# Layer 0's key pages turned on VectorE in 32x32 blocks: loads by quarters, new slot and query-tile order

## The chip, the cores and the metric

The kernel runs on one core of one Trainium2 chip. The metric is the device time of one launch in microseconds (us), given as the median of the runs. Engines are named as in the profile: PE (TensorE; PEld is its weight loads), DVE (VectorE), ACT (ScalarE), POOL (GpSimd) and SP (SyncE, which here issues nearly all DMAs). All arithmetic of the part that is changed is in float32.

## What is computed

Two layers of a decoder trunk run as one step for a prompt of 512 tokens and for a sample group of 8 sequences with 8 new tokens each. Every sample sequence has 1024 past tokens in 8 pages of 128, found through a page table. The change touches the attention of layer 0 only, where 8 forgetting ("fox") heads and 4 differential heads (two query/key halves each) attend side by side. Cut from the reference:

```python
def fox_diff_attend(qa, qb, cq, q_pos, ka, va, ck, kb, vb, k_pos, lam, subln0):
    causal = k_pos[None, :] <= q_pos[:, None]
    sa = einsum('bqhd,bkhd->bhqk', qa, ka) * scale
    sa = sa + (cq - ck)                      # sums of the log forget values
    oa = einsum('bhqk,bkhd->bqhd', softmax(where(causal, sa, -inf)), va)
    sb = einsum('bqhcd,bkhcd->bhcqk', qb, kb) * scale
    pb = softmax(where(causal, sb, -inf))
    ob = einsum('bhqk,bkhe->bqhe', pb[:, :, 0] - lam * pb[:, :, 1], vb)
    return concat(oa, rms_norm(ob, subln0) * (1 - LAMBDA_INIT))

# sample group, one sequence: 8 pages of keys and values (128 tokens x 1024), then the 8 new tokens
k_all = concat(cache_k[page_table], k_new); v_all = concat(cache_v[page_table], v_new)
```

A page of keys or values is 128 x 1024 float32, 512 KB. There are 64 of each.

## The kernel before

`FirstAttention` does this attention in 32 slots (the loop variable `x`), four to a sample sequence (`b, k = divmod(x, 4)`); the text calls four slots a batch. Each slot carries one unit of the prompt and a share of one sequence of the sample.

A unit is a pair of heads `p` and a query tile `qt` of 128 prompt tokens; its scores are (qt+1) x 128 wide. `QT_ORDER` sets the order of the query tiles in a pair. The first 16 units are "mixed" (differential heads: two score matrices are blended into one), the last 16 are fox heads (two score matrices each). For unit `x`, PE computes `scores(x)`, DVE the row maximum (`top`), ACT the exponentials (`exps`), DVE the reciprocal sums (`sums`); for mixed units POOL scales and DVE blends (`blend`). One slot later PE transposes the probabilities (`turn(x-1)`), ACT (and DVE, for a fox unit's second head) copies them out of PSUM (`head_out`), and PE multiplies them by the values (`weigh(x-1)`).

Of the sample, a slot takes in two key pages and two value pages. A key page arrives with tokens on the 128 partitions and features along the row. The score product needs features on the partitions, so `turn_keys(g)` lets PE transpose the page in eight 128x128 pieces into two PSUM banks (`RING`), and `keys_out(g)` copies them to SBUF, one bank by ACT and one by DVE. `score_page` then multiplies a turned page by the 128 query rows of the sequence (16 heads x 8 tokens) with 32-column tiles of PE, and `weigh_page` does the same for a value page with the transposed probabilities. The two RING banks also serve the transposes of probabilities, of the sample's probabilities (`turn_probs`) and of its output (`turn_o`).

SP issues the loads in one order: key page `g` waits until page `g-5` has been turned (five places), then value page `h = g - 11` waits until page `h-4` has been used (four places). Before each of them SP reads the page number from a table in SBUF. There are three places for turned keys.

The order of a slot on PE is written out by hand in `tensor`: scores, first key page turned, first value page, `turn(x-1)`, one page scored, second key page turned, second value page, another page scored, `weigh(x-1)`; the fourth slot of a batch scores four pages, the first none. After the last slot the last sequence's probabilities are turned and its eight value pages weighed, and the output projection of layer 0 follows.

Of the kernel before, what the change touches and what calls it, by code (L numbers as in the profile page):

```python
# [18 lines left out]
P = 128  # L19
# [8 lines left out]
KC = D_MODEL // P  # L28
# [40 lines left out]
def constant_table():  # L69
# [13 lines left out]
    row_head, row_query = i // DEC_SEQ, i % DEC_SEQ  # L83
# [4 lines left out]
    put("selections", selections)  # L88
    put("new_mask", np.where(h8[None, :] <= row_query[:, None], 0.0, NEG))
# [1246 lines left out]
class FirstAttention:  # L1336
    
    KEY_PLACES, VALUE_PLACES, TURNED_PLACES = 5, 4, 3
    QT_ORDER = (2, 1, 3, 0)
# [4 lines left out]
    def __init__(self, nc, K, mem, qp, kp, vp, qs, ks, vnew, retired, next_tile):  # L1344
# [3 lines left out]
                 "turned_a", "turned_b", "emptied_a", "emptied_b", "chain", "pool_chain",  # L1348
# [12 lines left out]
        self.knew, self.snew, self.st = sb("knew", [P, KC, DEC_SEQ]), sb("snew", [P, DEC_SEQ]), sb("st", [P, 2, 10])  # L1361
        self.squares = sb("squares", [P, DIFF, SEQ])
# [18 lines left out]
        self.fills_after_key = {}  # L1381
        self.fill_of_second_probs = {}
        self.fill_of_second_head = {}
# [21 lines left out]
    def tensor(self, pe):  # L1405
        K, S = self.K, self.S
        filled = [0, 0]
        turned, emptied = (S["turned_a"], S["turned_b"]), (S["emptied_a"], S["emptied_b"])

        def ring(x):  # L1410
            if filled[x]:
                pe.wait_ge(emptied[x], filled[x])
            filled[x] += 1
            return self.RING[x]
# [16 lines left out]
        def turn(u):  # L1431
            p, qt = self.units[u]
            for i in range(1 if self.mixed(u) else 2):
                bank = ring(i)
                if self.mixed(u):
                    pe.wait_ge(S["blended"], self.count(u + 1, True))
                for j in range(qt + 1):
                    ins = pe.transpose(bank[:, j * P:(j + 1) * P], self.probs[:, u % 2, i, j * P:(j + 1) * P], K.c("ident"))
                ins.then_inc(turned[i], 1)
                if i:  # L1440
                    self.fill_of_second_head[u] = filled[1]
            self.head_fills = (filled[0], filled[1])

        def weigh(u):
            p, qt = self.units[u]
            pe.wait_ge(emptied[0], self.head_fills[0])
            if not self.mixed(u):
                pe.wait_ge(emptied[1], self.head_fills[1])
# [18 lines left out]

        def turn_keys(g):
            pe.wait_ge(self.k_in[g % self.KEY_PLACES], 16 * (g // self.KEY_PLACES + 1))
            for x in range(2):  # L1470
                bank = ring(x)
                for c in range(4):
                    at = (4 * x + c) * P
                    ins = pe.transpose(bank[:, c * P:(c + 1) * P], self.keys[g % self.KEY_PLACES][:, at:at + P], K.c("ident"))  # L1474
                ins.then_inc(turned[x], 1)
            self.fills_after_key[g] = filled[1]
            self.key_fills[g] = (filled[0], filled[1])
# [9 lines left out]
        def score_page(b, j):  # L1487
# [10 lines left out]
            pe.wait_ge(emptied[0], self.key_fills[g][0])  # L1498
            pe.wait_ge(emptied[1], self.key_fills[g][1])
# [4 lines left out]
        def score_news(b):  # L1504
            news = ring(1)[:, 0:DEC_SEQ]
            pe.matmul(news, K.fox_sel[32:32 + 2 * FOX, :], self.bias_rows[:, PAST_LEN:KEYS], start=True, stop=True)
            score_into(news, lambda c: self.knew[:, c, :]).then_inc(turned[1], 1)

        def turn_probs(b):
            for half in range(2):  # L1510
                bank = ring(half)
                pe.wait_ge(S["s_exped"], 3 * b + (1, 3)[half])
# [3 lines left out]
                ins.then_inc(turned[half], 1)  # L1516
            self.probs_fills[b] = (filled[0], filled[1])
            pe.transpose(ring(1)[0:DEC_SEQ, 0:P], self.s_probs[:, PAST_LEN:KEYS], K.c("ident")).then_inc(turned[1], 1)
            self.fill_of_second_probs[b] = filled[1]
# [49 lines left out]
        for x in range(self.SLOTS + 1):  # L1569
            b, k = divmod(x, 4)  # L1570
            if k == 1 and b >= 2:
                turn_o(b - 2)
# [1706 lines left out]
```

## Time and profile before

| | us |
|---|---|
| median of 3 runs | 1894.41 (1892.2 to 1894.65) |
| the profiled execution, its own time | 1891.96 |
| its span, first to last instruction | 1890.2 |
| layer 0's attention: first key page issued to last value page weighed | 229.4 to 515.6 |
| PE busy over the span | 1707.6 (90%) |
| DVE, ACT, POOL busy over the span | 853.5, 603.2, 151.1 |
| mean granted TensorE clock | 0.957 |

The profile is one execution seen by the hardware profiler. A line of it names the source line, the engine, the operation, what is written and read, and how often; "idle before" is the time the engine stood still just ahead of such instructions, and the releaser is what ended it. PE's matmuls overlap, so the distance from one start to the next tells more than the length of one. TensorE's clock is granted at one of two levels, 1.00 (2.4 GHz) and 0.50 (1.2 GHz); a stretch in which it changed shows a value between. The DMA share is the mean busy share of the core's 16 DMA engines.

### The profile page before, as it was taken

To read this page: it belongs to the slowest core of one execution; us is meant where nothing else is said; L and a number is where in the kernel's file an instruction comes from. 1 tells how busy PE (TensorE), PEld (TensorE's weight loads), DVE (VectorE), ACT (ScalarE), POOL (GpSimd) and SP (SyncE) were. 2 spreads that over 40 slices of the span, in tenths; PEclk is the share of its full clock that TensorE was granted. 3 is DMA by queue.
4 is the path that set the end of the run, shared out by engine and by line. 5 is a ranking of instruction groups with operands and counts; after the bars stand their busy time and mean duration, and the time that the engine had idled before them with its cause. 6 is when DMAs were issued, how large, how long until landed. Compare 5 with 4: busy or idle time off the path is not lost. (4 is left out here: it accounts for less than half of the span.)

```text
span 1890.2 us, 32284 instructions
## 1 busy us (share of the span) xinstructions
PE 1707.6 (90%) x12454; PEld 1422.2 (75%) x12462; DVE 853.5 (45%) x1570; ACT 603.2 (32%) x1275; POOL 151.1 (8%) x303
## 2 busy tenths in 40 slices
PE   5999788998798999999998788687888999999998
PEld 3787565665478999799987576355457999889987
DVE  4446455445435322323224978985545232233323
ACT  3325344433223321112213344554333232112220
POOL 1222223111000000000000012110000000000000
PEclk9999899999898999999998899798999999999999
DMA  5232278766632222333321112101752322233221
GB/s 183 68 117 57 86 265 278 269 218 222 205 101 67 76 79 84 87 104 83 105 76 59 48 45 48 46 1 47 217 137 67 89 68 83 84 90 85 70 84 67
DMA packets 177043, 201.61 MB, mean 107 GB/s; under 512 B 21650, under 2 KB 131538, under 8 KB 176914
## 3 DMA queue, kind: packets, MB, share of 16 engines
q1 hardware_dynamic: 167634, 189.39, 32.6%
q10 hardware_dynamic: 9200, 10.24, 1.7%
q8 instruction: 81, 1.33, 0.3%
q14 instruction: 48, 0.39, 0.1%
q0 software_dynamic: 80, 0.26, 0.1%
HBM read 190.77 MB, written 9.08 MB: 106 GB/s over the span
## 5 line engine op out<-in xcount | busy, mean ns | idle before, releaser
L211 PE MATMUL ps<-feat_lo,w_hi 128*128 128x288 f32 x1408 | 416.5, 296 | 7.4 <-PEq L2451 3.8
L213 PE MATMUL ps<-feat_hi,w_hi 128*128 128x288 f32 x1408 | 416.5, 296 | 0.0
L212 PE MATMUL ps<-feat_hi,w_lo 128*128 128x288 f32 x1408 | 416.1, 296 | 0.0
L193 DVE TENSOR_TENSOR w_lo<-w_raw,w_hi 128x2048 fp32r<-128x2048 f32 x96 | 220.1, 2292 | 339.5 <-ACT w_hi L187 339.4
L187 ACT ACTIVATE w_hi<-w_raw 128x2048 fp32r<-128x2048 f32 x96 | 183.6, 1913 | 348.8 <-PE ps L219 334.9
L211 PEld LDWEIGHTS ps<-feat_lo,w_hi 128*128 128x128 f32 x1408 | 265.7, 189 | 8.6 <-issue 4.4
L212 PEld LDWEIGHTS ps<-feat_hi,w_lo 128*128 128x128 f32 x1408 | 265.7, 189 | 0.0
L213 PEld LDWEIGHTS ps<-feat_hi,w_hi 128*128 128x128 f32 x1408 | 265.5, 189 | 0.0
L2551 DVE TENSOR_TENSOR f_prod<-f_silu,ps 128x576 f32<-128x576 f32 x44 | 33.2, 754 | 361.1 <-ACT f_silu L2530 361.1
L211 PE MATMUL ps<-w_lo,feat_hi 128*128 128x512 f32 (+1 forms) x448 | 182.4, 407 | 13.5 <-DVE feat_lo L2403 5.5
L212 PE MATMUL ps<-w_hi,feat_lo 128*128 128x512 f32 (+1 forms) x448 | 177.9, 397 | 0.0
L213 PE MATMUL ps<-w_hi,feat_hi 128*128 128x512 f32 (+1 forms) x448 | 177.8, 397 | 0.0
L2530 ACT ACTIVATE f_silu<-ps 128x576 f32<-128x576 f32 x44 | 28.7, 652 | 429.6 <-PE ps L213 429.6
L212 PE MATMUL ps<-w_hi,f_act_lo 128*128 128x512 f32 x352 | 137.0, 389 | 0.0
L211 PE MATMUL ps<-w_lo,f_act_hi 128*128 128x512 f32 x352 | 137.0, 389 | 0.0
L213 PE MATMUL ps<-w_hi,f_act_hi 128*128 128x512 f32 x352 | 136.9, 389 | 0.0
L211 PEld LDWEIGHTS ps<-w_lo,feat_hi 128*128 128x128 f32 x448 | 88.6, 198 | 32.3 <-issue 14.4
L213 PEld LDWEIGHTS ps<-w_hi,feat_hi 128*128 128x128 f32 x448 | 87.9, 196 | 17.9
L212 PEld LDWEIGHTS ps<-w_hi,feat_lo 128*128 128x128 f32 x448 | 88.6, 198 | 16.1
L1474 PE MATMUL ps<-const,places 128*128 128x128 f32 x512 | 70.7, 283 | 13.4 <-ACT a_probs_t L1618 8.6
L213 PEld LDWEIGHTS ps<-w_hi,f_act_hi 128*128 128x128 f32 x352 | 66.1, 188 | 13.7
L211 PEld LDWEIGHTS ps<-w_lo,f_act_hi 128*128 128x128 f32 x352 | 66.1, 188 | 13.6
(340 smaller groups left out, 2386.4 us busy)
## 6 DMA issues: line engine op xcount, KB each, us to landing
places<-in_cache_l_k_dram SPq DMA_DIRECT2D x64, 512.0 KB, 4.5
places<-in_cache_l_v_dram SPq DMA_DIRECT2D x64, 512.0 KB, 5.1
w_raw<-in_w_gate_dram SPq DMA_DIRECT2D x44, 512.0 KB, 4.0
w_raw<-in_w_up_dram SPq DMA_DIRECT2D x44, 512.0 KB, 5.3
w_raw<-in_w_in_dram SPq DMA_DIRECT2D x18, 1024.0 KB, 5.2
w_raw<-in_w_down_dram SPq DMA_DIRECT2D x16, 1024.0 KB, 5.1
s_kslot<-in_cache_l_k_dram SPq DMA_DIRECT2D x56, 128.0 KB, 2.8
w_raw<-in_w_down_dram SPq DMA_DIRECT2D x8, 768.0 KB, 4.3
```

Of the source, the lines that this page charges most:

```text
L187: act.activation(self.K.w_hi[:, n % 2, :], self.K.w_raw[:, n % 2, :], ACT.Copy).then_inc(self.split_hi, 1)
L193: dve.tensor_tensor(self.K.w_lo[:, n % 2, :], self.K.w_raw[:, n % 2, :], self.K.w_hi[:, n % 2, :].bitcast(F32), ALU.subtract).then_inc(sel ...
L211: pe.matmul(out, lhs[0], rhs[1], start=start, stop=False)
L212: pe.matmul(out, lhs[1], rhs[0], start=False, stop=False)
L213: return pe.matmul(out, lhs[0], rhs[0], start=False, stop=stop)
L1474: ins = pe.transpose(bank[:, c * P:(c + 1) * P], self.keys[g % self.KEY_PLACES][:, at:at + P], K.c("ident"))
L2530: act.activation(silu[:, x, :, :], K.ps[:, 4 * x:4 * x + 2, 0:H], ACT.Silu).then_inc(S["silu_ok"], 1)
L2551: dve.tensor_tensor(prod[:, x, :, :], silu[:, x, :, :], K.ps[:, 4 * x + 2:4 * x + 4, 0:H], ALU.mult)\
```

## The change

PE no longer transposes the key pages. A page is fetched by four DMAs, one for each quarter of its 1024 features, so that the 32 partitions 32a to 32a+31 hold tokens 0 to 31 of each group of 32 and, along the row, the four groups of tokens with the 256 features of quarter `a` each. One VectorE instruction then transposes all 32x32 blocks of the page from SBUF to SBUF. The queries and the new keys are brought into the same order of features (`q_rows`, `k_rows`, spread once by ACT and POOL at the start), and the 128 query rows stand in another order of heads, which a permuting copy by ACT (four instructions for each half of `probs_out`) undoes for the probabilities, and a small matmul with the constant `swap` for the factors (`swap_factor`, `factor_out`). All probabilities leave PSUM by ACT now. The order of a slot on PE becomes scores, `turn(x-1)`, two value pages, two pages scored, `weigh(x-1)`. The query tiles of a pair run 0, 1, 2, 3. The squares for the differential heads' norm take a used part of `kp` as their place.

The core of the diff:

```diff
-    QT_ORDER = (2, 1, 3, 0)
+    QT_ORDER = (0, 1, 2, 3)
...
-        def turn_keys(g):
-            pe.wait_ge(self.k_in[g % self.KEY_PLACES], 16 * (g // self.KEY_PLACES + 1))
-            for x in range(2):
-                bank = ring(x)
-                for c in range(4):
-                    at = (4 * x + c) * P
-                    ins = pe.transpose(bank[:, c * P:(c + 1) * P], self.keys[g % self.KEY_PLACES][:, at:at + P], K.c("ident"))
-                ins.then_inc(turned[x], 1)
...
             if x < self.SLOTS:
                 scores(x)
-                turn_keys(2 * x)
+            if x:
+                turn(x - 1)
             before = b - 2 if k == 0 else b - 1
             first = (6, 0, 2, 4)[k]
             if before >= 0:
                 weigh_page(before, first)
-            if x:
-                turn(x - 1)
-            if x < self.SLOTS and k:
-                score_page(b, 2 * k - 2)
-            if x < self.SLOTS:
-                turn_keys(2 * x + 1)
-            if before >= 0:
                 weigh_page(before, first + 1)
...
             if x < self.SLOTS and k:
+                score_page(b, 2 * k - 2)
                 score_page(b, 2 * k - 1)
...
+        def probs_out(b):
+            nonlocal emptied
+            for half in range(2):
+                dst = self.pt[:, 4 * half:4 * half + 4, :].rearrange("p j (x y q) -> p y (j x) q", x=4, y=4)
+                src = self.RING[half].rearrange("p (j y x q) -> p y j x q", j=4, y=4, x=4)
+                emptied += 1
+                act.wait_ge(S["act_turned"], emptied)
+                for y in range(4):
+                    ins = act.activation(dst[:, y].rearrange("p (j x) q -> p j x q", j=4), src[:, y], ACT.Copy)
+                ins.then_inc(S["act_emptied"], 1)
...
-        def keys_out(g):
+        def turn_keys(g):
+            dve.wait_ge(self.k_in[g % self.KEY_PLACES], 64 * (g // self.KEY_PLACES + 1))
             if g >= self.TURNED_PLACES:
                 dve.wait_ge(S["page_scored"], g - self.TURNED_PLACES + 1)
-            bank = filled()
-            dve.tensor_copy(self.turned[g % self.TURNED_PLACES][:, 4:8, :], bank.rearrange("p (c n) -> p c n", n=P))\
-               .then_inc(S["emptied_b"], 1)
+            src = self.keys[g % self.KEY_PLACES].rearrange("p (g c n) -> p g c n", g=4, c=KC)
+            dst = self.turned[g % self.TURNED_PLACES].rearrange("p c (g n) -> p g c n", g=4)
+            dve.transpose(dst, src).then_inc(S["keys_turned"], 1)
...
         def load_key(g):
             if g >= self.KEY_PLACES:
-                sp.wait_ge(S["turned_b"], self.fills_after_key[g - self.KEY_PLACES])
-            sp.dma_start(self.keys[g % self.KEY_PLACES], page(K.cache_l0_k, g)).then_inc(self.k_in[g % self.KEY_PLACES], 16)
+                sp.wait_ge(S["keys_turned"], g - self.KEY_PLACES + 1)
+            src = page(K.cache_l0_k, g).rearrange("(g k) (a n) -> a k g n", g=4, a=4)
+            dst = self.keys[g % self.KEY_PLACES].rearrange("p (g n) -> p g n", g=4)
+            for a in range(4):
+                sp.dma_start(dst[32 * a:32 * a + 32], src[a]).then_inc(self.k_in[g % self.KEY_PLACES], 16)
```

How the instructions stand is shown at three places. First SP, at the end of a key page and the value page behind it (`places` holds key and value pages, `pages` is the page table, ISA rows compute addresses). Before:

```order
L1910 DMA places<-in_cache_l_k_dram 128x1024
L1902 TENSOR_LOAD pages
L1902 ISA x2
L1922 ISA
L1922 DMA places<-in_cache_l_v_dram 128x1024
```

Now, where the first row is the last of four such DMAs of one key page, each with an ISA row ahead of it:

```order
L1932 DMA places<-in_cache_l_k_dram 32x4x256
L1921 TENSOR_LOAD pages
L1921 ISA x2
L1944 ISA
L1944 DMA places<-in_cache_l_v_dram 128x1024
```

The page number is still read once for a page; three DMAs and three address computations have been added to each key page.

Second PE, slot 6 (a mixed unit in the third slot of a batch; `kp`, `qp` are the prompt's keys and queries, `a_probs` the probabilities, `free_49` the sample's queries or turned probabilities). Before:

```order
L1423 MATMUL ps<-kp,qp 128x512 x2
L1428 MATMUL ps<-causal_bf,ident_bf 128x128 x2
L1474 MATMUL ps<-const,places 128x128 x8
L1531 MATMUL ps<-places,free_49 32x256 x4
L1438 MATMUL ps<-const,a_probs 128x128 x2
L1483 MATMUL ps<-places,free_49 32x128 x8
L1464 MATMUL ps<-a_probs_t,vp 128x128 x2
```

That piece leaves out the slot's second key page, second value page and second scored page, which stand as a second run of the L1474, L1531 and L1483 rows ahead of L1464. Now the whole slot:

```order
L1424 MATMUL ps<-kp,qp 128x384 x2
L1429 MATMUL ps<-causal_bf,ident_bf 128x128 x2
L1441 MATMUL ps<-const,a_probs 128x128 x2
L1528 MATMUL ps<-places,free_49 32x256 x8
L1471 MATMUL ps<-places,free_49 32x128 x16
L1463 MATMUL ps<-a_probs_t,vp 128x128 x2
```

The 16 key transposes of the slot are gone, the probabilities are turned right behind the scores, and the narrow products stand together.

Third DVE in the same slot (`a_minus` the row maxima, `a_scale` the reciprocal sums). Before:

```order
L1777 SCALAR_TENSOR_TENSOR a_probs<-a_probs,a_scale 128x256
L1762 TENSOR_REDUCE a_minus<-ps 128x2
L1749 COPY places<-ps 128x512 x2
L1767 RECIPROCAL a_scale<-a_total 128x2
L1771 TENSOR_SCALAR a_scale<-a_scale,minus_lam 128x1
```

Now:

```order
L1798 SCALAR_TENSOR_TENSOR a_probs<-a_probs,a_scale 128x256
L1783 TENSOR_REDUCE a_minus<-ps 128x2
L1779 STREAM_TRANSPOSE places<-places 128x4x8x32 x2
L1788 RECIPROCAL a_scale<-a_total 128x2
L1792 TENSOR_SCALAR a_scale<-a_scale,minus_lam 128x1
```

Two copies of half a page out of PSUM have become two transposes of a whole page inside SBUF, at the same place in the order.

## Rows read from the trace of the kernel before

**Rows 1.** Windows: busy us of PE, PEld, DVE, ACT, POOL; clock, DMA share, GB/s.

```profile
258.00:349.00 91.00, 82.95 (x1031) 55.19 (x1022) 47.37 (x116) 40.41 (x117) 25.71 (x66) 1.00 0.77 263
349.00:497.00 148.00, 138.10 (x1653) 93.33 (x1645) 69.36 (x167) 56.33 (x160) 19.88 (x73) 0.98 0.66 216
```

**Rows 2.** Timeline of PE, one mixed slot: start, length, line, operation, count.

```profile
303.60 1.13 PE L1423 MATMUL ps<-kp,qp 64*128 64x512 f32 x4
...
304.79 1.05 PE L1474 MATMUL ps<-const,places 128*128 128x128 f32 x8
305.76 0.64 PE L1531 MATMUL ps<-places,free 128*32 128x256 f32 x8
...
307.39 1.06 PE L1474 MATMUL ps<-const,places 128*128 128x128 f32 x8
```

**Rows 3.** Timeline of PE: last scores of a batch, first of the next, end.

```profile
257.25 1.08 PE L1483 MATMUL ps<-places,free 128*32 128x128 f32 x32
258.26 0.92 PE L1423 MATMUL ps<-kp,qp 64*128 64x384 f32 x4
...
497.30 0.61 PE L1531 MATMUL ps<-places,free 128*32 128x256 f32 x8
```

**Rows 4.** Waits of SP, 200 to 540: for whom, us, times, longest.

```profile
SPq L1902 <- PE ps L1474: 111.3, 56, 8.1
...
SPq L1902 <- PE ps L1531: 16.5, 7, 3.8
```

**Rows 5.** Timeline of SP: issues of key (L1910) and value (L1922) pages.

```profile
229.38 5.28 SPq L1910 DMA_DIRECT2D places<-in_cache_l_k_dram  x5
...
275.69 0.33 SPq L1910 DMA_DIRECT2D places<-in_cache_l_k_dram  x1
276.79 0.33 SPq L1922 DMA_DIRECT2D places<-in_cache_l_v_dram  x1
...
475.96 0.33 SPq L1910 DMA_DIRECT2D places<-in_cache_l_k_dram  x1
```

**Rows 6.** Groups by line, 225 to 545: busy us, mean ns, idle before.

```profile
L1474 PE MATMUL ps<-const,places 128*128 128x128 f32 x512 | 70.7, 283 | 13.4 <-ACT a_probs_t L1618 8.6 <-DMA places<-in_cache_l_k_dram 4.6
L1749 DVE COPY places<-ps 128x512 f32<-128x512 f32 x64 | 44.0, 688 | 62.0 <-PE ps L1474 62.0
```

**Rows 7.** SP issues without a page read between; last: ns min/median/max, first and last start.

```profile
1316.66 3.99 SPq L2027 DMA_DIRECT2D s_kslot<-in_cache_l_k_dram  x8
...
542.02 0.37 SPq L180 DMA_DIRECT2D w_raw<-in_w_gate_dram  x1
542.43 0.58 SPq L180 DMA_DIRECT2D w_raw<-in_w_up_dram  x1
...
L180 SPq DMA_DIRECT2D w_raw<-in_w_out_dram x4: 618/648/1257, 1396.7 to 1399.4; - x4
```

**Rows 8.** Windows of 1 us: DMA share and GB/s are the last columns.

```profile
109.00:110.00 1.00, 1.00 (x6) 0.81 (x6) 0.97 (x3) 0.00 (x0) 1.00 (x1) 1.00 1.02 385
246.00:247.00 1.00, 0.69 (x6) 0.34 (x4) 1.00 (x2) 0.60 (x1) 0.00 (x0) 1.00 1.03 410
1404.00:1405.00 1.00, 1.00 (x6) 0.84 (x5) 0.00 (x0) 0.00 (x0) 0.00 (x0) 1.00 1.06 225
```

**Rows 9.** Page, part 6: DMA issues, KB each, median us to landing.

```profile
places<-in_cache_l_k_dram SPq DMA_DIRECT2D x64, 512.0 KB, 4.5
```

**Rows 10.** Groups by line, 225 to 545: DVE over 1024 elements a partition.

```profile
L1762 DVE TENSOR_REDUCE a_minus<-ps 128x2 f32<-128x1024 f32 x8 | 9.8, 1225 | 7.9 <-PE ps L1428 7.9
```

**Rows 11.** Groups by line, 225 to 545: ACT copies of probabilities out of PSUM.

```profile
L1618 ACT ACTIVATE a_probs_t<-ps 128x512 f32<-128x512 f32 x8 | 4.8, 597 | 8.7 <-PE ps L1438 8.7
...
L1618 ACT ACTIVATE a_probs_t<-ps 128x128 f32<-128x128 f32 x8 | 2.2, 277 | 0.0
```

**Rows 12.** Windows at the attention's end, PE waiting for value pages.

```profile
506.00:509.00 3.00, 0.64 (x8) 0.16 (x8) 0.00 (x0) 0.00 (x0) 0.00 (x0) 1.00 1.02 368
510.00:513.00 3.00, 0.00 (x0) 0.00 (x0) 0.00 (x0) 0.94 (x1) 0.00 (x0) 0.51 1.01 393
```

More of the change, by code:

```diff
@@ L1406, in tensor, with ring @@
         K, S = self.K, self.S
[L1407 to L1413, printed above, removed]
+        fills = {"act": 0, "dve": 0}
+        holder = [None, None]
+        def ring(x, who):
+            if holder[x] is not None:
+                pe.wait_ge(S[holder[x][0] + "_emptied"], holder[x][1])
+            fills[who] += 1
+            holder[x] = (who, fills[who])
             return self.RING[x]
@@ L1515, in turn_probs, with turn_new_probs, swap_factor @@
                                        K.c("ident"))
[L1516 to L1519, printed above, removed]
+                ins.then_inc(S["act_turned"], 1)
+            self.probs_fills[b] = fills["act"]
+        def turn_new_probs(b):
+            bank = ring(0, "act")
+            pe.wait_ge(S["s_exped"], 3 * b + 3)
+            pe.transpose(bank[0:DEC_SEQ, 0:P], self.s_probs[:, PAST_LEN:KEYS], K.c("ident")).then_inc(S["act_turned"], 1)
+            self.new_fills[b] = fills["act"]
+        def swap_factor(b):
+            bank = ring(1, "dve")
+            pe.wait_ge(S["weighted"], b + 1)
+            pe.matmul(bank[:, 0:1], K.c("swap"), self.st[:, b % 2, 9:10], start=True, stop=True).then_inc(S["dve_turned"], 1)
         def weigh_page(b, j):
@@ L1570, in tensor @@
             b, k = divmod(x, 4)
-            if k == 1 and b >= 2:
+            if k == 1 and b:
+                turn_new_probs(b - 1)
+                swap_factor(b - 1)
+            if k == 2 and b >= 2:
                 turn_o(b - 2)
@@ L1667, in scalar @@
                 exps(x)
-                keys_out(2 * x + 1)
+            if k == 0 and b:
+                sample_exps(b - 1)
             if self.SQUARES <= x < self.SQUARES + DIFF:
@@ L1683, in gpsimd, with spread_keys @@
             pool.sem_clear(range(lo, hi))
+        def spread_keys():
+            for a in range(4):
+                for half in range(2):
+                    for x in range(2):
+                        at = HEAD_DIM * half + 32 * x
+                        s.ok(pool.tensor_copy(self.k_rows[32 * a:32 * a + 32, 2 * half + x::4, :],
+                                              self.ks[at:at + 32, 2 * a:2 * a + 2, :]))
+                        s.wait()
+            pool.sem_inc(S["k_spread"], 1)
         def queries(b):
@@ L1871, in vector @@
             if x < self.SLOTS:
-                keys_out(2 * x + 1)
+                turn_keys(2 * x + 1)
             if k == 3 and b < DEC_BATCH:
```

173 lines of the change are left out of this document (85 added, 88 removed).

## The prediction, made before the changed kernel was run

> **What bounds the kernel now.** I read the windows by stage first, for the stage that the change touches. Layer 0's attention runs from 229.4 to 515.6, and PE is busy for 82.95 of 91 us in its mixed part and for 138.10 of 148 in its fox part, at a clock of 1.00 and 0.98 [rows 1]. ACT and DVE are at 44 and 52% there at most, and the DMA engines at 66 to 77%. So PE sets the pace of the slots. The timeline of PE then shows what a slot consists of. The two runs of eight key transposes take 1.0 us each to the next start (304.79 to 305.76) in a slot of 6.4 us, and the narrow products stand between them [rows 2]. The seven batches between the end of the first (258.26) and the end of the slot loop (497.30) take 34.1 us each [rows 3].
>
> The waits of SP come next, because the change gives SP more to do. SP stood still for 111.3 us until key places came free and for 16.5 us until value places did [rows 4]. That is all the slack it has: from its first key at 229.4 to its last at 476.0 it issues 64 key and 52 value pages, 1.10 us apart where nothing holds it up (275.69 to 276.79) [rows 5]. It runs ahead of its users now: the last key page is issued 21 us before the slot loop ends [rows 3, 5].
>
> **The change, part by part.**
>
> *Key transposes leave PE.* 512 matmuls go, eight for each of 64 pages at 1.0 us: 64 us of PE's path [rows 2, 6]. If PE remained the bound, the loop would end at 433 instead of 497. What is late next decides.
>
> *Four DMAs for a key page.* SP gets 192 more issues, each with an address computation. No row has a 32-partition quarter. The nearest is the later loads of pages of 128 partitions by 1 KB, without a number read between: eight in 3.99 us, thus (3.99 - 0.33) / 7 = 0.52 us apart [rows 5, 7]. The ends are 0.41, two weight loads with fixed addresses (542.02 to 542.43), and 0.90, four loads to 64 partitions (2.7 us between the first and the last of four) [rows 7]. I take 0.52, since those loads also have a page address and the same number of runs. A key page then costs SP 1.10 + 3 x 0.52 = 2.67 us, and its work up to the last key is 64 x 2.67 + 52 x 1.10 + some 14 small loads at 0.5 = 171 + 57 + 7 = 235 us. Without any wait the last key is issued at 229.4 + 235 = 464. It has to land (4.5 us) [rows 9], be turned (1.2) and scored (1.1 for the last four pages) [rows 3]: the loop ends at about 471, 26 us earlier. The lead of 21 us is used up; SP has become the pacemaker, at 8 x (2.67 + 1.10) + 1 = 31 us a batch. That PE, at (91 / 3 - 8) = 22 us a mixed and (148 / 4 - 8) = 29 a fox batch, is faster from then on is worth nothing [rows 1].
>
> *Where the quarters land.* 512 KB over all partitions move at 410 GB/s in runs of 4 KB and at 385 in runs of 2 KB; two loads of 64 partitions each, behind each other, move at 225 [rows 8]. So the loss is by partitions and not by length of run. A quarter's rate lies between 225 (no further loss) and 225 x 225 / 385 = 131 (the same factor once more). I take 225, the row itself: a key page takes 2.3 us, and 64 x 2.33 + 52 x 1.28 + small loads is 218 us, under SP's 235. On the slow side 131 makes it 4.0 us, and then DMA sets the pace; that is a rival. The Trainium skill speaks against this part of the change ("SBUF — State Buffer", Door 1: The DMA port swizzle): a transfer reaches only the ports of its partitions, 64 partitions have half of them, and 32 partitions have as many as 64. The row of 225 agrees for 64 partitions; for 32 no run here shows it. By that rule the sum stays as it is.
>
> *Turning on DVE.* Two copies of 0.69 us in a slot give way to two transposes of 1024 elements a partition [rows 6]. No row has one. The nearest is the row maximum over 1024 elements, 1.23 us [rows 10]; I bound the transpose by 0.69, as little as today's copy of half a page, and by twice the row, 2.45. At 1.23 DVE has 47.37 / 3 + 8 x 0.54 = 20 us of work in a mixed batch, at 2.45 30 us: both under 31, so it doesn't set the pace by its sum [rows 1]. But it waits in order: in a slot `turn_keys` now stands between `top(x)` and `sums(x)`, and while DVE waits for a landing key, `sums(x)`, POOL's scale, the blend and with them PE's `turn(x)` are queued behind it. From the landing of a slot's second key to the next slot's first scored page I count 1.2 + 0.4 + 1.6 + 0.8 + 0.6 + 1.1 + 0.6 and some 0.6 of hand-over, 6.9 us, against 7.8 that SP needs for a slot. It fits, with 0.9 to spare.
>
> *Slot order and query tiles.* `turn(x-1)` loses the key transposes that covered its wait for the blend; this is inside the 6.9. Narrow products in one run save PE some gaps; nothing, as long as SP paces. With the order 0, 1, 2, 3 the last unit is 512 wide instead of 128: two ACT copies of 0.60 in a row for one of 0.28 beside DVE's, and more matmuls; and the sample's probabilities leave PSUM in eight pieces on ACT instead of one copy on ACT beside one on DVE [rows 11]. These lie behind the last slot on the path to the end: 0.9 + 1.3 + about 1 = 3 us.
>
> *At the start* the queries and keys are spread by 16 small copies each on ACT and POOL while the first keys are still on their way; the first batch is paced by eight keys at 2.67 us in either case, and I cost the spreading at nothing. If it weren't covered it would be some 4 us, once.
>
> *Sum.* -26 for the loop, +3 for the end, +3 for places where SP's work doesn't flow evenly (the batch that also holds the squares is longer than 31 us even without its transposes): -20. The profiled execution's 1891.96 becomes 1872; the median of the runs is 2.4 above that execution, so I forecast **1874**.
>
> **The rivals.**
>
> *SP issues at 0.41.* SP's last key would be issued 192 x 0.11 = 21 us earlier still, at 443; the DMA sum (229.4 + 2 + 218 = 449) would then be later and set the pace: 15 us are left of it, 1859. If the quarters also lost nothing, all 21 would count, 1853. For it: fixed addresses show 0.41. Against: each quarter has its own address computation.
>
> *The gain is spent.* At 0.62 an issue SP's work grows by 19 us and the forecast is back at 1893, no change; at 0.70 by 34 us, 1908. For it: the 64-partition loads show 0.62 to 1.26 for one issue [rows 7].
>
> *Slower: quarters at 131 GB/s.* One mechanism: each DMA feeds a quarter of the partitions, and the loss seen from 128 to 64 partitions comes again from 64 to 32. The DMA work up to the last key is 64 x 4.0 + 52 x 1.28 + 3 = 326 us, the loop ends near 564, and the time is 1891.96 + 67 + 3 + 2.4 = 1964. It decides from the point at which a key page takes longer than SP's 2.67 us (196 GB/s), and turns the gain into a loss at (34.1 - 8 x 1.28 - 0.4) / 8 = 2.9 us (179 GB/s). For it: the first halving cost 41%. Against: the same 16 DMA engines would have to lose again.
>
> *Slower: the clock.* PE will wait for keys in most slots. When it waited for value pages at the end, the clock was 1.00 in one stretch with 0.64 us of work in 3 and 0.51 soon after [rows 12]. If it fell in half of the batches, PE's 22 to 29 us there would become up to 44 to 58, and the time would be about 1891.96 - 20 + 4 x 18 = 1945. Against: the forecast leaves PE 70 to 90% busy, in pieces. The Trainium skill ("TensorE: Matmul & The Clock Gate", HAM oscillation) tells of a kernel whose short bursts between DMA waits lost the fast clock again and again; rows 12 agree for the end, and no run here shows it in the slots.
>
> **How the numbers follow.** The measurement tells a change from none beyond about 0.2%, 3.8 us. Forecast, with what lies between 0.45 and 0.58 an issue: 56%. Issues at 0.41 or so: 13%. Gain spent, within 0.2%: 10%. Slower by a little, up to 1908, dear issues or DVE at its upper end: 8%. Quarters at 131 or so: 8%. Clock: 5%. So faster 0.69, same 0.10, slower 0.21. The range runs from 1853 to 1908 and leaves out the last two cases and a little below.
>
> **What would show it.** The key matmuls are gone from PE and its busy share of the stage falls to about three quarters; SP's waits for places fall from 128 us to under 30; four issues of a key page stand 0.52 us apart; the DMA rate falls to about 225 GB/s within key pages; the transposes take about 1.2 us; DVE waits for key DMAs; batches last 31 us. I am wrong if SP still waits much (then PE, DVE or the blend sets the pace), if key pages land later and later behind their issue (then the quarters do), or if the clock is at 0.50 in the slots.

## The result, and the profile after

The changed kernel takes 1911.02 us (median of 5 runs, 1900.39 to 1917.42) against 1893.42 for the kernel before: a ratio of 1.0089 (95% interval 1.0053 to 1.0126), so 0.9% slower, where 1874 was forecast with a range up to 1908. Its profiled execution took 1900.39 us with a span of 1898.6, the shortest of the five; its runs spread over 17 us, those of the kernel before over 3. One execution of e12 (7995 us, the only slow one here) is left out of that run's median.

In the windows of the two parts of the stage (columns as in [rows 1]) PE has the room that the change was to give it, 66 of 91 and 115 of 148 us busy. What is at its top now is the DMA share, above 1 in both parts, and yet the rate behind it is 238 and 243 GB/s, lower in the first part than the 263 of before at a share of 0.77.

```profile
258.00:349.00 91.00, 66.22 (x695) 39.85 (x687) 52.39 (x103) 28.58 (x110) 18.48 (x26) 0.79 1.04 238
349.00:497.00 148.00, 115.09 (x1426) 72.22 (x1426) 76.15 (x153) 47.98 (x175) 13.86 (x23) 0.91 1.06 243
```

The DMA view of the changed kernel, 258 to 497 us (issues, KB each, median us from issue to landing), shows the same from the other side. A quarter page takes longer to land than a whole page did [rows 9], and a value page, whose DMA nobody changed, 9.1 us. The last row is that of the value pages in the kernel before, over the same stretch: 5.0 us.

```profile
q1 hardware_dynamic: 39795, 57.32, 104.6%
...
places<-in_cache_l_k_dram SPq DMA_DIRECT2D x220, 128.0 KB, 6.0
places<-in_cache_l_v_dram SPq DMA_DIRECT2D x52, 512.0 KB, 9.1
...
places<-in_cache_l_v_dram SPq DMA_DIRECT2D x54, 512.0 KB, 5.0
```

SP's timeline (start, length, line, operation, count) answers [rows 5]: the first 19 quarters take 11.69 us, 0.62 each with their page reads, and where nothing holds SP up, four quarters (L1932) and a value page (L1944) come every 3.70 us (283.10 to 286.80).

```profile
229.46 11.69 SPq L1932 DMA_DIRECT2D places<-in_cache_l_k_dram  x19
...
283.10 1.81 SPq L1932 DMA_DIRECT2D places<-in_cache_l_k_dram  x4
285.68 0.35 SPq L1944 DMA_DIRECT2D places<-in_cache_l_v_dram  x1
286.80 1.81 SPq L1932 DMA_DIRECT2D places<-in_cache_l_k_dram  x4
...
483.70 1.85 SPq L1932 DMA_DIRECT2D places<-in_cache_l_k_dram  x4
```

The waits of SP up to the last key page, 229 to 486 us (for whom, us, times, longest), answer [rows 4]: 19.1 us are left.

```profile
SPq L1921 <- DVE places L1779: 18.6, 12, 5.4
SPq L1921 <- PE ps L1528: 0.5, 2, 0.3
```

So two things look nearly full in the slots, SP's issues and, by its share, the DMA queue. The timeline of PE at the end of the first batch and at the end of the loop answers [rows 3]. The first scores of the second batch start at 258.28, as before (258.26). The last key page is scored 6 us later than before, and from the end of the first batch's scores to the end of the last it is 35.0 us a batch, (503.26 - 258.36) / 7, for 34.1. The last pair of transposes of the stage starts at 523.16; the last row is the same pair in the kernel before, 517.39.

```profile
257.71 0.65 PE L1471 MATMUL ps<-places,free 128*32 128x128 f32 x16 [0.75 <-DVE places L1779]
258.28 0.49 PE L1424 MATMUL ps<-kp,qp 64*128 64x128 f32 x4
...
502.18 1.08 PE L1471 MATMUL ps<-places,free 128*32 128x128 f32 x32
...
523.16 0.66 PE L1544 MATMUL ps<-const,a_o_sb 128*128 128x128 f32 x2 [0.70 <-DVE a_o_sb L1846]
...
517.39 0.66 PE L1547 MATMUL ps<-const,a_o_sb 128*128 128x128 f32 x2 [0.70 <-DVE a_o_sb L1826]
```

The groups by line (229 to 520 us) answer [rows 6, 10]: the transposes on DVE take 1.23 us each, and DVE waits 12.1 us for key pages. PE now stands still for 44.3 us ahead of its products with value pages, until these land; the last row shows those products in the kernel before, with 6.4 us. So it is the value pages, more than the key pages, that come too late.

```profile
L1779 DVE STREAM_TRANSPOSE places<-places 128x1024 f32<-128x1024 f32 x64 | 78.5, 1234 | 58.8 <-PE ps L1471 46.7 <-DMA places<-in_cache_l_k_dram 12.1
...
L1528 PE MATMUL ps<-places,free 128*32 128x256 f32 x504 | 41.8, 423 | 44.4 <-DMA places<-in_cache_l_v_dram 44.3
...
L1531 PE MATMUL ps<-places,free 128*32 128x256 f32 x512 | 41.2, 399 | 6.4 <-DMA places<-in_cache_l_v_dram 6.4
```

### The profile page after: what moved, and what is told of

It reads as the page before. It is cut to its first block and busy times, and to the rows that moved or that the text cites. A ratio compares the mean times of both kernels' runs of the same rounds, so it can differ in the third digit from the quotient of the medians.

```text
span 1898.6 us, 31580 instructions
## 1 busy us (share of the span) xinstructions
PE 1671.0 (88%) x11958; PEld 1386.5 (73%) x11966; DVE 872.4 (46%) x1546; ACT 587.8 (31%) x1307; POOL 138.8 (7%) x215
## 5 line engine op out<-in xcount | busy, mean ns | idle before, releaser
L1779 DVE STREAM_TRANSPOSE places<-places 128x1024 f32<-128x1024 f32 x64 | 78.5, 1234 | 58.8 <-PE ps L1471 46.7
L1528 PE MATMUL ps<-places,free 128*32 128x256 f32 x512 | 42.9, 426 | 44.6 <-DMA places<-in_cache_l_v_dram 44.5
```

The source lines that it names most:

```text
L1528: ins = pe.matmul(self.SO[self.rows4[i], :], self.pt[:, j, self.rows4[i]], values[:, i * 2 * P:(i + 1) * 2 * P], start=(j == 0), stop=False)
L1779: dve.transpose(dst, src).then_inc(S["keys_turned"], 1)
```

## The experiments

Theory A: DMAs of 32 partitions hold the whole DMA queue down, the value pages behind them too. Theory B: it is the runs of 1 KB. Theory C: it is the four issues on SP. Theory D: it is the waits in the new slot order, with the clock that falls in them. "Last score" below is the start of the last matmul that scores a key page, in the profiled execution; the kernel before has it at 497.2, the changed one at 503.0. Ratios are against runs of the kernel before on the same chip, with 95% intervals. In e2 to e5, e9 and e13 to e16 the features of a page stand where the queries don't expect them: these runs measure time and compute something else. The edits are shortened to the lines that matter.

| run | us | ratio | last score |
|---|---|---|---|
| e1 cut by tokens | 2076.1 | 1.097 (1.095 to 1.098) | 678.5 |
| e2 one DMA a page | 1843.9 | 0.974 (0.972 to 0.976) | 447.2 |
| e3 32 partitions, 4 KB | 1904.9 | 1.006 (1.004 to 1.007) | 505.3 |
| e4 before, with quarters | 1909.7 | 1.009 (1.007 to 1.010) | 511.8 |
| e5 128 partitions, 1 KB | 1887.3 | 0.996 (0.995 to 0.998) | 487.4 |
| e6 order 0, 2, 1, 3 | 1899.8 | 1.003 (1.001 to 1.004) | 498.1 |
| e7 quarters from two queues | 1891.3 | 0.998 (0.996 to 1.000) | 499.8 |
| e8 old query order | 1908.3 | 1.007 (1.005 to 1.010) | 512.6 |
| e9 both lifted | 1850.6 | 0.977 (0.975 to 0.978) | 458.5 |
| e10 values by ACT | 1876.6 | 0.992 (0.990 to 0.994) | 484.6 |
| e11 values by ACT, 0213 | 1867.7 | 0.987 (0.985 to 0.988) | 465.1 |
| e12 two queues, dealt 02/13 | 1894.2 | 1.000 (0.998 to 1.001) | 492.3 |
| e13 64 partitions | 1920.1 | 1.014 (1.012 to 1.016) | 523.2 |
| e14 64, alternating | 1917.8 | 1.012 (1.010 to 1.014) | 524.5 |
| e15 64, values by ACT | 1887.9 | 0.997 (0.996 to 0.998) | 494.3 |
| e16 64 alternating, values by ACT | 1877.8 | 0.991 (0.990 to 0.993) | 485.5 |

### e1 to e4: is it the quarters, and what of them?

e1, e2 and e3 change only the loads of the changed kernel (and the count that DVE waits for, where it is one DMA); e4 puts the changed kernel's loads into the kernel before.

```diff
 # e1                                  (dst is [128, 4, 256], src is [a, k, g, n])
-    sp.dma_start(dst[32 * a:32 * a + 32], src[a])
+    sp.dma_start(dst[:, i, :], src[:, :, i, :])
 # e2
+    sp.dma_start(self.keys[g % self.KEY_PLACES], page(K.cache_l0_k, g))
 # e3
+    sp.dma_start(keys[32 * a:32 * a + 32, :], page[32 * a:32 * a + 32, :])
 # e4, in the kernel before
-    sp.dma_start(self.keys[g % self.KEY_PLACES], page(K.cache_l0_k, g))
+    for a in range(4):
+        sp.dma_start(dst[32 * a:32 * a + 32], src[a])
```

> The changed kernel, but a key page's four DMAs are cut by tokens instead of by features: DMA i fetches the 32 tokens 32i to 32i+31 for all four feature quarters, so that each DMA writes all 128 partitions, one run of 1 KB in each. Same four issues, same 128 KB a DMA, same runs of 1 KB, same result. Theory A (32 partitions are what holds the DMA queue at about 240 GB/s): the queue moves faster, SP's issues at 3.7 us for a key and a value page set the pace, about 31 us a batch, and the time is 1865 to 1880. Theory B (runs of 1 KB hold the queue down, whatever the partitions): as the changed kernel, 1905 to 1917. Theory C (four issues for a page, on SP or in the queue): 1905 to 1917 too. Theory D (the waits of PE on DVE and the blend in the new slot order, with the clock that falls in them): 1905 to 1917 too.

> The changed kernel, but a key page is fetched by one DMA over 128 partitions with runs of 4 KB, as in the kernel before; features and tokens then stand in other places than the queries expect, so the output isn't the reference's, while every instruction on the other engines stays. Theory A and B: the DMA queue moves at about 385 to 410 GB/s again and SP issues 128 pages at 1.10 us; what is left is PE at 22 to 29 us a batch with its waits for DVE, 1835 to 1865. Theory C: the same, 1835 to 1865; only here it is the first of the runs that is faster. Theory D: 1900 to 1917, nothing gained.

> The changed kernel, but a key page's four DMAs write 32 partitions each with one run of 4 KB in each partition (32 whole tokens a DMA) instead of four runs of 1 KB; the order of tokens and features is then not what the queries expect, so the output isn't the reference's. Same four issues, same 128 KB a DMA, same partitions. Theory A (partitions): as the changed kernel, 1900 to 1917, and the DMA rate of the slots stays near 240 GB/s at a share above 1. Theory B (runs of 1 KB): 1865 to 1880. Theory C: 1905 to 1917. Theory D: 1905 to 1917.

> The kernel before, with PE's key transposes and its slot order, but its key pages fetched by the changed kernel's four DMAs (32 partitions, four runs of 1 KB in each); the features of a page then stand in other places than the queries expect, so the output isn't the reference's. Theories A and B: the queue is held at about 240 GB/s, 35 to 36 us a batch instead of 34.1, so slower than the kernel before, 1900 to 1920. Theory C (SP): 31 us of issues a batch lie under PE's 34, so 1890 to 1897. Theory D: 1890 to 1897.

e1 lies 159 us above the highest range that was given for it and says nothing on A or B, because its cut brought another limit. The windows show a DMA share of 0.28 and 0.40, so nothing is full there; SP's timeline shows that the first 17 issues took 21.61 us, 1.27 each with their page reads instead of 0.62. The Trainium skill ("DMA: Bandwidth & Descriptors", Why a DMA increments its semaphore by 16 and not by 1) says that a DMA is spread over as many engines as divide the slowest dimension of both sides; on e1's source side that is the four feature quarters, so 4 of 16. The share of 0.28 agrees with a quarter; the rows don't show the engines one by one.

```profile
229.00:258.00 29.00, 10.58 (x86) 6.15 (x86) 8.31 (x13) 4.75 (x16) 7.88 (x23) 0.50 0.28 95
258.00:349.00 91.00, 42.75 (x385) 25.20 (x384) 31.90 (x55) 15.50 (x57) 11.60 (x16) 0.63 0.40 130
```

```profile
228.95 21.61 SPq L1932 DMA_DIRECT2D places<-in_cache_l_k_dram  x17
```

e2 rules out D as the main cause: with the quarters gone and nothing else changed on the engines, the last score comes 50 us earlier than in the kernel before (497.2 to 447.2), as expected by A, B and C. Its windows show PE at 75.65 of 91 and a rate of 295 GB/s at a share of 0.84.

```profile
258.00:349.00 91.00, 75.65 (x950) 47.43 (x950) 64.34 (x125) 36.68 (x145) 20.44 (x31) 0.92 0.84 295
```

e3 rules out B: with runs of 4 KB in 32 partitions the time falls by 6 us of the 31 to 46 that B needed, and its windows stay at 241 and 234 GB/s with a DMA queue that is nearly full.

```profile
258.00:349.00 91.00, 67.18 (x715) 40.23 (x714) 51.74 (x102) 28.36 (x110) 17.82 (x26) 0.77 0.94 241
349.00:497.00 148.00, 118.38 (x1365) 75.62 (x1368) 74.01 (x151) 47.80 (x174) 13.82 (x23) 0.85 0.98 234
```

e4 is the plainest of the runs. In its windows (the same two parts) PE still turns the keys, 136.75 of 148 us busy, and yet the time is that of the changed kernel, 1909.7 against 1911.0: with quarters loaded like this it makes no difference whether PE turns the pages or DVE does. C or D alone would have had it at 1890 to 1897.

```profile
258.00:349.00 91.00, 78.11 (x917) 51.93 (x908) 44.00 (x109) 35.80 (x104) 24.19 (x65) 0.96 0.99 237
349.00:497.00 148.00, 136.75 (x1600) 91.46 (x1592) 67.16 (x165) 55.51 (x159) 22.10 (x75) 0.97 1.04 233
```

### e5 and e7: each of two limits alone; e9: neither

e5 keeps the four issues of 128 KB and the runs of 1 KB, but lets each DMA write all partitions. e7 keeps the quarters and takes half of their issues from SP. e9 is e5 with the value pages issued by ACT.

```diff
 # e5
+    src = page(K.cache_l0_k, g).rearrange("k (a n) -> k a n", a=4)
-    sp.dma_start(dst[32 * a:32 * a + 32], src[a])
+    sp.dma_start(dst[:, a, :], src[:, a, :])
 # e7: SP issues a in (0, 1); in ACT's loop, at the start of a slot, for two pages:
+    act.wait_ge(S["keys_turned"], g - self.KEY_PLACES + 1)
+    for a in (2, 3):
+        act.dma_start(dst[32 * a:32 * a + 32], src[a]).then_inc(self.k_in[g % self.KEY_PLACES], 16)
 # e9, e10, e11, e15, e16: in ACT's loop, at the start of slot x, for h = 2x-8 and 2x-7
+    act.wait_ge(S["value_used"], h - self.VALUE_PLACES + 1)
+    act.dma_start(values, K.cache_l0_v[ds(m, 1), :, :].rearrange("a k d -> (a k) d")).then_inc(landed, 16)
```

> The changed kernel, but each of a key page's four DMAs writes all 128 partitions with one run of 1 KB in each (a quarter of every token's features; partitions lie outermost on both sides). Features and tokens then stand in other places than the queries expect, so the output isn't the reference's. Same four issues on SP, same 128 KB a DMA, same runs of 1 KB. Theory A (32 partitions hold the DMA queue): the queue moves as fast as in e2, SP's issues at 3.7 us for a key and a value page set the pace, and the time is 1860 to 1880. Theory C (SP: 222 us of issues between the first and the last key, and 32 us of waits on top of them): nothing changes for SP, 1900 to 1915.

> The changed kernel, but from the sixth key page on ACT issues the quarters 2 and 3 from its own queue at the start of the next slot, and SP only 0 and 1; the same DMAs to the same partitions, the same result. SP's work falls by about 1 us for each of 59 pages, ACT gets about 1.7 us of issue a page. Theory C (SP is the pacemaker): 1850 to 1885. Theory A (32 partitions are the limit whoever issues them): the DMA share in the slots stays at 1 and the rate at 240 GB/s, 1900 to 1915; if the two queues overlap DMAs of different partition groups, the rate rises above 260 GB/s and the time falls to 1850 to 1885 by A too, so the rate and the share decide between them.

> e5 (four DMAs of 128 partitions for a key page; features and tokens stand in other places than the queries expect, so the output isn't the reference's) with the value pages of the first seven batches issued by ACT from its own queue, so that SP issues only the key pages. Theory A+C (two limits, each close to the other: DMAs of 32 partitions allow some 238 GB/s, and SP's issues take 3.7 us for a key and a value page; the changed kernel has both, e5 and e7 one each): with both lifted the time comes near that of e2, 1840 to 1865. If something else held e5 at 1887 (the waits of DVE and PE in the slot order, the clock), it stays at 1880 to 1890.

e5 fell between A's 1860 to 1880 and C's 1900 to 1915. Its windows show a DMA queue with room again, 0.79 and 0.82:

```profile
258.00:349.00 91.00, 66.15 (x732) 39.38 (x730) 54.36 (x106) 29.15 (x112) 18.91 (x27) 0.83 0.79 247
349.00:497.00 148.00, 127.74 (x1585) 81.30 (x1585) 80.95 (x171) 54.08 (x198) 12.59 (x22) 0.88 0.82 256
```

But SP has none. It waits 5 us in all up to the last key page; by its timeline the four issues of that page end at 475.4, and the last score follows 12 us later.

```profile
SPq L1921 <- DVE places L1779: 2.8, 3, 2.3
SPq L1921 <- PE ps L1528: 2.6, 3, 2.0
```

```profile
473.51 1.91 SPq L1932 DMA_DIRECT2D places<-in_cache_l_k_dram  x4
```

e7 is the reverse. It came out below the 1900 to 1915 that A gave it, but the rate stays where A put it, at 237 and 239 GB/s with shares of 1.02 and 1.00. SP waits 79 us for places up to the last key page, so it is no limit.

```profile
258.00:349.00 91.00, 69.30 (x710) 40.41 (x711) 52.14 (x101) 28.55 (x111) 17.18 (x26) 0.77 1.02 237
349.00:497.00 148.00, 124.94 (x1429) 80.72 (x1432) 77.40 (x156) 50.54 (x180) 13.82 (x23) 0.84 1.00 239
```

```profile
SPq L1934 <- DVE places L1792: 78.6, 31, 11.0
```

But 1891 isn't the price of the DMA work by itself, for ACT now pays for the issues. From 258 to 480 us it stands 56 us ahead of its copies of a unit's result (L1643), which the profile puts down to issuing, and quarters 2 and 3 of a page start only when ACT comes to them in its own order. What this cost was not separated.

```profile
ACT att L1643 <- issue: 56.3, 14, 5.7
```

So A and C are both right, each for a part: lifting the partitions gains 24 us (1911 to 1887), halving the quarters on SP 20. With the partitions and SP's load both lifted, e9 gains 60 and comes within 7 us of e2. The run beside e9 that lifts SP's load alone is not e7 but e10 below, which moves the same value pages to ACT: 34 us. The two gains, 24 and 34, add up to 58 of the 60, so here neither limit hides the other.

### e6 and e8 to e12: order, query tiles, and a faster version

```diff
 # e6, e11
-    for a in range(4):
+    for a in (0, 2, 1, 3):
 # e8
-    QT_ORDER = (0, 1, 2, 3)
+    QT_ORDER = (2, 1, 3, 0)
 # e12: as e7, with SP on a in (0, 2) and ACT on a in (1, 3)
```

> The changed kernel with a key page's quarters issued in the order 0, 2, 1, 3 of their partition groups instead of 0, 1, 2, 3; the result is the same. Theory A in the form that a pair of neighbouring groups (0 and 1, 2 and 3) shares what is short: if two DMAs of one queue overlap, the alternation helps, 1870 to 1900; if each DMA drains before the next starts, nothing changes, 1900 to 1917. Theory C (SP): 1900 to 1917.

> The changed kernel with the query tiles of a pair in the order 2, 1, 3, 0 again; the result is the same. If the end behind the last slot (a 512-wide unit last instead of a 128-wide one) costs what I put down for it, about 2 us, and the order has no other effect: 1905 to 1912, about 2 us below the changed kernel. If the order 0, 1, 2, 3 evens out the slots (or unevens them, with two wide units behind each other), the difference is 5 us or more, to either side.

> The changed kernel with the value pages of the first seven batches issued by ACT; key pages by SP in four DMAs of 32 partitions each, order 0, 1, 2, 3; the result is the same. SP's work falls from 3.7 to about 2.6 us for a key and a value page. Theory A+C: the DMA limit remains, rate 238 GB/s at a share of 1, so as e7, 1885 to 1900. If SP alone had been the limit: 1850 to 1875.

> e10 with a key page's quarters in the order 0, 2, 1, 3; the result is the same. In e6 this order lowered the DMA share from about 1.05 to 0.97 at the same rate, and the landing of a quarter from 5.7 to 4.5 us, so by theory A it raises the limit of the DMA queue (from 3.05 to about 2.7 us a key page by the share): with SP relieved too, 1865 to 1885, faster than the kernel before. If the order acted only on waiting and not on the limit: as e10, 1885 to 1900.

> e7 with the quarters dealt otherwise: SP issues 0 and 2, ACT 1 and 3 (in e7 SP 0 and 1, ACT 2 and 3); the result is the same. If neighbouring DMAs of one queue should reach different partition halves (as e6 suggests), this is faster than e7: 1870 to 1885, with the rate above 245 GB/s. If the dealing makes no difference once two queues run beside each other: as e7, 1885 to 1898.

e6 gained 11 us, at the edge of what either reading expected. e8 is 2.7 us below the changed kernel, inside the spread of both, so the order of the query tiles costs at most a few us. e6 does not gain by a higher rate: its windows have 238 GB/s from 258 to 349 us and 239 from 349 to 485, the changed kernel's 238 and 241. e10 was better than A expected (1877 against 1885 to 1900): the same DMAs, with the value pages in ACT's queue, move at 260 GB/s instead of 240. e11, with the order 0, 2, 1, 3 on top, moves at 281 to 283, and at 1867.7 us it is the fastest version here that computes what the kernel before does, 1.3% below it.

The waits from 258 to 480 us show what moving the value pages did. The first two rows are the changed kernel's, the others e10's: PE hardly waits for value pages any more, and DVE waits for key pages instead. So e10's 34 us are not SP's time alone; the value pages also no longer stand in one queue behind the quarters.

```profile
PE ps L1528 <- DMA places<-in_cache_l_v_dram: 34.4, 17, 4.5
DVE places L1779 <- DMA places<-in_cache_l_k_dram: 3.3, 1, 3.3
...
PE ps L1528 <- DMA places<-in_cache_l_v_dram: 7.0, 7, 2.8
DVE places L1788 <- DMA places<-in_cache_l_k_dram: 27.5, 13, 4.7
```

The windows below are those of e10, then of e11, then of e9, two stretches each; the second ends at 460, where e9 leaves the loop.

```profile
258.00:349.00 91.00, 69.95 (x769) 42.38 (x761) 57.55 (x112) 29.82 (x113) 19.68 (x27) 0.80 1.08 261
349.00:460.00 111.00, 94.01 (x1150) 60.57 (x1150) 61.09 (x122) 38.17 (x137) 11.46 (x18) 0.86 1.08 259
```

e11, the same stretches:

```profile
258.00:349.00 91.00, 70.56 (x848) 43.05 (x852) 62.44 (x116) 31.85 (x119) 22.07 (x33) 0.86 1.04 283
349.00:460.00 111.00, 101.98 (x1278) 64.85 (x1270) 67.05 (x138) 46.78 (x170) 8.79 (x16) 0.92 1.06 281
```

e9, the same stretches:

```profile
258.00:349.00 91.00, 72.38 (x884) 44.14 (x884) 64.47 (x124) 33.48 (x126) 23.47 (x33) 0.87 0.89 303
349.00:460.00 111.00, 106.00 (x1376) 70.41 (x1376) 69.68 (x145) 46.71 (x170) 8.79 (x16) 0.92 0.85 283
```

e12 was expected to gain over e7 by the same order, and did not (1894 and 1891), though its profile has 254 GB/s in the first part (239 in the second). Where the quarters of one page come from two queues, how they are dealt made no difference to the time; why, the runs don't tell.

### e13 to e16: the number of partitions, or which of them?

e13 and e14 write 64 partitions by 2 KB in each DMA, e13 with the same half twice in a row, e14 with alternating halves; e15 and e16 are these two with the value pages issued by ACT.

```diff
 # e13, e15: ((0, 0), (0, 1), (1, 0), (1, 1));  e14, e16: ((0, 0), (1, 0), (0, 1), (1, 1))
+    for half, part in order:
+        rows, cols = slice(64 * half, 64 * half + 64), slice(512 * part, 512 * part + 512)
+        sp.dma_start(keys[rows, cols], page[rows, cols])
```

> The changed kernel, but each of a key page's four DMAs writes 64 partitions with one run of 2 KB in each, in the order lower half, lower half, upper half, upper half; features and tokens then stand in other places than the queries expect, so the output isn't the reference's. Same four issues, same 128 KB a DMA. If 64 partitions are no better than 32 (two neighbouring groups share what is short): as the changed kernel and e3, 1900 to 1912, DMA share of the slots 0.95 or more at some 240 GB/s. If 32 partitions lose against 64: towards e5, 1885 to 1897, with a share below 0.9.

> e13 with the halves in the order lower, upper, lower, upper; the output isn't the reference's for the same reason. If what counts is that neighbouring DMAs reach different halves: below e13 by about the 11 us that the order 0, 2, 1, 3 gained in e6, 1885 to 1900. If the order doesn't count for DMAs of 64 partitions: as e13, within 4 us.

> e13 (key pages by four DMAs of 64 partitions with runs of 2 KB, lower half twice, then upper half twice; the output isn't the reference's for the same reason) with the value pages of the first seven batches issued by ACT, as in e9 and e10. SP's own work is then about 3.25 us a key page, 208 us in all, so SP isn't the limit. If 64 partitions are like 32 (neighbouring groups share what is short): as e10 or e11, 1865 to 1880, rate about 260 GB/s at a share above 1. If they are like 128: as e9, 1848 to 1858, rate about 290 GB/s at a share below 0.95.

> e15 with the halves alternating; the output isn't the reference's for the same reason. If neighbouring DMAs should reach different halves: faster than e15 by about the 9 us between e10 and e11. If 64 partitions lose nothing: as e15, within 4 us.

e13 and e14 decide nothing: SP's timeline of e13 shows 4.36 us for a key and a value page (289.87 to 294.23), and SP sets the pace by itself.

```profile
289.87 2.46 SPq L1933 DMA_DIRECT2D places<-in_cache_l_k_dram  x4
293.10 0.36 SPq L1945 DMA_DIRECT2D places<-in_cache_l_v_dram  x1
294.23 2.44 SPq L1933 DMA_DIRECT2D places<-in_cache_l_k_dram  x4
```

With SP relieved, 64 partitions (1888 and 1878) are no better than 32 (e10 and e11, 1877 and 1868) and far from 128 (e9, 1851); that they are even 10 us worse may come from their longer issues and was not separated. Changing the order from the same half twice to alternating halves is worth 9 us for 32 partitions and 10 for 64. In the window of the second stretch (e15 first, then e16) the rate rises from 253 to 273 GB/s, as from e10 to e11 it rose from 259 to 281.

```profile
349.00:460.00 111.00, 96.99 (x1157) 62.96 (x1157) 62.10 (x120) 39.16 (x138) 11.87 (x18) 0.85 0.98 253
```

e16, the same stretch:

```profile
349.00:460.00 111.00, 99.07 (x1260) 63.41 (x1258) 69.44 (x141) 42.26 (x148) 14.75 (x24) 0.91 1.03 273
```

The Trainium skill ("SBUF — State Buffer", Door 1: The DMA port swizzle), which the prediction cited for the point that 32 partitions reach as many ports as 64, agrees with these runs: DMAs of 64 partitions are no faster than DMAs of 32. That alternating halves help is shown by the runs alone, and for the rate only where ACT issues the value pages; with all issues on SP the order gained 11 us for 32 partitions (e6) and 2 for 64 (e14), the latter within the spread. With alternating halves e11's rate is still under e9's in the first stretch, 283 against 303 GB/s, and why the mix of quarter and whole DMAs falls as low as 240 is not settled.

## Why the prediction was wrong, step by step

**PE is the bound, and turning costs it 64 us: right.** e2, whose loads hinder least, has the last score 50 us earlier and runs at 1844. In the changed kernel PE's busy time in the two windows fell by 40 us (221.05 to 181.31). Of the 64 us, 56 stood in these windows (448 of the 512 transposes); that the rest of PE's work ran at a lower clock, 0.79 and 0.91, fits the difference, but it was not measured by itself.

**218 us of DMA work under SP's 235, and so at no cost: wrong, and this is the step that failed.** The prediction took the row of 64 partitions, 225 GB/s, for the rate of a quarter, and priced a value page behind it at an undisturbed 1.28 us. e5 lifts nothing but the partitions and gains 24 us; with the value pages on ACT they are worth 26 (e10 to e9). The 116 pages of 0.524 MB in 218 us would be 279 GB/s; the changed kernel moved 238 to 243, and the wait that grew is PE's for value pages, which land in 9.1 us instead of 5.0. No run gives a quarter's own price. As an estimate, with a value page still at 1.28 us, 240 GB/s leave 2.9 us for a key page, the point at which the prediction has the gain spent; e10's 260 leave 2.6, and e11's 282 leave 2.3, the prediction's own figure. So the price hangs on the order of the DMAs and on the queue of the value pages, and the sum had a term for neither. The rival "quarters at 131" named what would be short, but not how: it has the loss come again from 64 to 32 partitions, and e15 and e16 show none there. Its price (4.0 us, 1964) was too high.

**SP's issues: the size was right, "without any wait" was not.** A key and a value page take 3.70 us, 3.77 were put down. From the first key to the end of the last page's issues (229.5 to 485.5) SP spends 256 us, of which 19 are waits: 237 of its own work against 235. e5, where SP sets the pace, gives 1887 instead of 1874: 5 us of waits, some 5 more of work, and 12 us from the last issue to the last score where 7 were put down. That alone is above the forecast by 13 us of the 37.

**The later of two: wrong as a rule here.** The sum took the later of SP's work and the DMA work, 235 against 218, so that lifting the DMA limit should have gained nothing. The four runs that go together are 1911 with both limits, 1887 without the partitions' (e5), 1877 with the value pages on ACT (e10) and 1851 with both changes (e9): the gains add up. The traces show one way in which they add. SP, the pacemaker, waits for places too, 19 us in the changed kernel and 5 in e5, and its last issue ends 10 us later (485.5 against 475.4); from there to the last score it takes 17.5 us instead of 12. That makes up the 15.6 us between the last scores of these two profiles (503.0 and 487.4). The medians lie 24 us apart, since the changed kernel's profiled execution is its fastest.

**Turning on DVE: right.** 1.234 us against 1.23. DVE waits 12.1 us for key DMAs and 46.7 for PE to free a place of turned keys, which fits PE's wait for value pages, since PE frees the places; e2 and e9 show that the order of work on DVE leaves room for 1844 and 1851.

**End and start.** The end was put at +3 us and costs nothing: from the last score to the last transpose start it is 20.4 us in both kernels (497.2 to 517.6, 503.0 to 523.4). The spreading at the start was put at nothing and costs nothing: the second batch begins at 258.28 instead of 258.26 [rows 3].

**The clock.** The rival had it at 0.50 in half of the batches. It did fall: in the changed kernel's windows of 10 us it is 0.50 in one, after a stretch in which PE was busy for 4.25 of 10 us, and 1.00 in a later one.

```profile
280.00:290.00 10.00, 4.25 (x48) 2.19 (x52) 3.59 (x5) 1.92 (x5) 0.38 (x1) 0.67 0.97 267
290.00:300.00 10.00, 9.27 (x101) 5.63 (x93) 6.05 (x11) 2.59 (x9) 3.80 (x6) 0.50 1.10 250
...
400.00:410.00 10.00, 6.87 (x75) 3.85 (x73) 4.79 (x11) 6.40 (x28) 0.55 (x3) 1.00 1.08 237
```

In e2 the two parts of the stage have 0.92 and, up to the last score at 447, 0.97, where the kernel before has 1.00 and 0.98 [rows 1]. The lower clock goes along with the waits; what it costs beside them was not measured by a run of its own.

## What to carry to other kernels

A transfer cut to a part of the partitions is priced by the whole queue behind it: read what a mixed stretch moves, not the best row of each kind, and count all that stands in the same queue. When two resources come out as close in a sum as 218 and 235 us, the later one need not be the time: here both cost, and lifting one gave back its own part only. Test each alone and then both, with the same change in each pair, or the parts can't be told apart. Moving one stream of transfers to another engine's queue, and letting neighbouring transfers reach different halves of the partitions, was here worth 43 us (e11) of the 67 that loading by quarters cost (e2).

## What the runs showed of the hardware that was not expected

The time that SP needs to issue a DMA depends on its form more than on its bytes, 128 KB each time: 0.50 us for 32 partitions with four runs of 1 KB and 0.72 for 64 partitions with one run of 2 KB (from 3.70 and 4.36 us for a key and a value page, less two page reads with an issue at 1.10 [rows 5], by three), and 1.27 with the page reads for e1's form, whose source has the four quarters outermost. With the value pages in ACT's queue, the order of otherwise equal DMAs in SP's moved the rate by 20 GB/s, for 32 and for 64 partitions; with all pages in SP's queue (e6) it left the rate as it was. And a DMA share of 1 does not mean the full rate: 240, 260 and 282 GB/s all stood beside shares of 1.04 to 1.08, while 303 stood beside 0.89.
